# The last block's expert rows added by a 0/1 product, other blocks' rows during it, and z1 with its contraction outside

## What is computed

```
for l in range(2):
    h = rmsnorm(x, norm_mix[l])
    z = h @ w_in[l]                       # first 640 of its columns: "z1"; the other 800: "z2"
    ...                                   # two attentions, gates
    x = x + mix @ w_out[l]
    h = rmsnorm(x, norm_ffn[l])
    grp = argmax(h @ w_group + b_group)   # one group a token, so one row of results a token
    ...                                   # top 2 of the group's 8 experts, weights
    x = x + sum over the 2 experts of wt * ((silu(h @ w1[e]) * (h @ w3[e])) @ w2[e])
return rmsnorm(x, norm_final)             # x: 512 tokens x 1024
```

## Time and profile before

| | us |
|---|---|
| median of 3 runs (lowest, highest) | 2060.18 (2056.29, 2061.72) |
| profiled execution | 2053.19 |
| its span from the first to the last recorded instruction | 2051.5 |
| PE busy | 1942.0 |
| DVE, ACT busy | 1412.4, 1205.5 |
| mean DMA rate over the span | 252 GB/s |

### The profile page before, as it was taken

How to read it: one execution, slowest core, us unless ns; L and a number is a source line. 1 busy time by engine, 2 the same in 40 slices (tenths; PEclk the granted TensorE clock), 3 DMA queues, 4 the chain that set the end, 5 groups by cost and what they waited for, 6 DMA issues and landing times.

```text
span 2051.5 us, 27023 instructions
## 1 busy us (share of the span) xinstructions
PE 1942.0 (95%) x9266; PEld 1576.4 (77%) x9266; DVE 1412.4 (69%) x1792; ACT 1205.5 (59%) x1510; POOL 162.6 (8%) x175
## 2 busy tenths in 40 slices
PE   8979999999999999999688899999999999999994
PEld 6867777787888888888578677777888888888883
DVE  4344444468999899889544344436689998999895
ACT  4444444247777777777444444433477777777773
POOL 0000000022110111011000000000301100110010
PEclk9999999999999999999889999999999999999997
DMA  4234113549999999999421631135699999999992
GB/s 147 81 94 116 59 36 102 207 150 391 382 370 374 379 378 369 382 381 378 147 97 60 138 91 42 42 110 194 211 391 391 370 360 385 385 369 375 377 362 89
DMA packets 157960, 500.66 MB, mean 244 GB/s; under 512 B 22288, under 2 KB 38672, under 8 KB 157872
## 3 DMA queue, kind: packets, MB, share of 16 engines
q1 hardware_dynamic: 146192, 459.70, 60.8%
q0 software_dynamic: 11680, 39.80, 6.5%
HBM read 486.79 MB, written 29.63 MB: 252 GB/s over the span
## 4 chain that ended last, share of the span: by engine, by line
PE 90%; DVE 4%; ACT 2%; DMA 1%; issue 1%; POOL 0%; POOLq 0%; DVEq 0%; ACTq 0%; SPq 0%
PE ps L1449 27%; PE ps L1451 25%; PE ps L1450 25%; PE ps L1668 3%; PE ps L1600 2%; PE ps L1604 2%; PE ps L1654 1%; PE ps L1798 1%; DVE wl L1017 1%; ACT wh L666 1%; DVE wl L1012 1%; PE ps L1759 1%; PE ps L1713 1%; PE ps L1497 1%; PE ps L1771 1%
## 5 line engine op out<-in xcount | busy, mean ns | idle before, releaser
L1012 DVE TENSOR_TENSOR wl<-raw,wh 128x2048 fp32r<-128x2048 f32 (+1 forms) x402 | 907.5, 2279 | 186.3 <-ACT wh L665 183.7
L665 ACT ACTIVATE wh<-raw 128x2048 fp32r<-128x2048 f32 (+1 forms) x406 | 753.9, 1883 | 75.8 <-PE ps L1451 67.6
L1449 PE MATMUL ps<-wh,xgh 128*128 128x512 f32 x1024 | 414.2, 405 | 0.0
L1451 PE MATMUL ps<-wh,xgl 128*128 128x512 f32 x1024 | 402.4, 393 | 0.0
L1450 PE MATMUL ps<-wl,xgh 128*128 128x512 f32 x1024 | 401.3, 392 | 0.0
L1451 PEld LDWEIGHTS ps<-wh,xgl 128*128 128x128 f32 x1024 | 192.2, 188 | 43.5
L1450 PEld LDWEIGHTS ps<-wl,xgh 128*128 128x128 f32 x1024 | 192.8, 188 | 37.7
L1449 PEld LDWEIGHTS ps<-wh,xgh 128*128 128x128 f32 x1024 | 192.5, 188 | 37.9 <-issue 0.2
L1449 PE MATMUL ps<-wh,hth 128*128 128x512 f32 x512 | 200.9, 392 | 2.0 <-DVE htl L1035 2.0
L1451 PE MATMUL ps<-wh,htl 128*128 128x512 f32 x512 | 200.7, 392 | 0.0
L1450 PE MATMUL ps<-wl,hth 128*128 128x512 f32 x512 | 200.7, 392 | 0.0
(11 more groups left out here) (294 smaller groups left out, 2675.8 us busy)
## 6 DMA issues: line engine op xcount, KB each, us to landing
raw<-in_w SPq DMA_DIRECT2D x512, 512.0 KB, 6.1
raw<-in_w SPq DMA_DIRECT2D x128, 1024.0 KB
raw<-in_w_gate SPq DMA_DIRECT2D x16, 1024.0 KB
xslots<-zrow POOLq DMA_DIRECT2D x2, 6240.0 KB, 36.1
xg<-xslots POOLq DMA_DIRECT2D x16, 520.0 KB, 6.9
raw<-in_w_out SPq DMA_DIRECT2D x8, 1024.0 KB
raw<-in_w_in SPq DMA_DIRECT2D x8, 800.0 KB
raw<-in_w_oa SPq DMA_DIRECT2D x4, 1024.0 KB
```

Source lines behind the costliest of these rows:

```text
L665: return nc.scalar.activation(dst, src, ACT.Copy)
L1012: return V.tensor_tensor(dst, src, hi.bitcast(F32), ALU.subtract)
L1449: MM(dst, lh, rh, start=first, stop=False)
L1451: return MM(dst, ll, rh, start=False, stop=last)
```

## The change

The result rows of the last block no longer go through DRAM. `place` holds each token's slot less 896 (the last block's first slot). In the last block DVE compares a row 0..127 with it (`selection`), which gives a 0/1 matrix token x slot (`sel`); PE transposes it to bank 7 and ACT copies it to `selt`. At the block's end ACT rounds the 128 x 1024 rows to `yh` (`y_high`), DVE subtracts to `yl` (`y_low`), and PE multiplies `selt` with both, which puts each row at its token (`y_product`: 16 products of 128 x 512 into all eight banks). DVE adds the banks to `xl` (`add_half`).

The other blocks' rows are still written to `yrows`, which is now set to zero by a DMA in the attention part. During the last block GpSimd reads them tile by tile into `yb`, and DVE adds each to `xl` (`earlier_rows`), one after expert 3, 4, 5 and 6's first `up` unit; the next tile is read when the one before is added. `hi_unit(0)` and `lo_unit(0)` ahead of the last copies are gone.

z1 now runs k outside and the five column groups inside, and waits by k: `first_high(k)` and `first_low(k)` split one k of a unit and signal `hk_done`, `lk_done`. The transposed halves are renumbered: half c of tile t goes to bank 4c+t, and k 0 to 3 need only the halves c = 0. In layer 0 PE does 5 instead of 8 products with `ident`.

```diff
+                pool.dma_start(yrows, zrow[0, 0:D].partition_broadcast(T)).then_inc(S["zero_in"], 16)
...
-                n_blocks = blocks(pool, move_block)
-                pool.wait_ge(S["gath_in"], n_blocks * 16)
-                hold(n_blocks, 0)
-                nc.gpsimd.memset(ib[:, :], 0).then_inc(S["moe_done"], 1)
...
+                with pool.Fori(0, NG - 1) as b:
+                    move_block(b, b)
...
-                    pool.dma_start(y8[:, t, :], tiles(yrows)[:, t]).then_inc(S[f"y8_in{t}"], 16)
...
+                    if t:
+                        pool.wait_ge(S["xm_done"], t)
+                    pool.dma_start(yb[:, :], tiles(yrows)[:, t]).then_inc(S["y8_in"], 16)
...
+            def first_high(k):
+                n = first_unit(k)
+                if k == plan[n][1]:
+                    hi_room(n, 0)
+                for (gain, dst), (_, src) in zip(first_pieces(k, hi_at(n)), first_pieces(k, raws[rl_place(n)], True)):
+                    last = hi_part(dst, src, gain)
+                last.then_inc(S["hk_done"], 1)
...
+            def y_high(b):
+
+                act.wait_ge(S["used_m"], b * NU + NU)
+                for h in range(2):
+                    nc.scalar.activation(yh[:, h * 512:(h + 1) * 512], ps[5 + h][:, :], ACT.Copy
+                                         ).then_inc(S["yh_done"], 1)
...
+                if l:
+                    first_high(0)
                 square(0)
                 square(1)
                 root(0)
                 square(2)
                 root(1)
-                turned_high(0)
-                square(3)
-                root(2)
-                turned_high(1)
+                if l == 0:
+                    square(3)
+                    root(2)
+                turned_high(0, 0)
+                if l:
+                    square(3)
+                    root(2)
+                turned_high(0, 1)
                 root(3)
-                turned_high(2)
-                split_to(1)
-                turned_high(3)
+                turned_high(1, 0)
+                turned_high(2, 0)
+                if l == 0:
+                    first_high(0)
+                turned_high(3, 0)
+                first_high(1)
+                first_high(2)
+                for t in range(1, NT):
+                    turned_high(t, 1)
+                for k in range(3, KD):
+                    first_high(k)
                 split_to(U_Z1[1] + 1)
                 if l == 0:
                     act.wait_ge(trig_in, 2)
@@ -918,23 +962,25 @@
...
+                        if u == ("up", 4, 1) and not prepare:
+                            act.wait_ge(S["selt_ps"], b - (NG - 2))
+                            nc.scalar.activation(selt[:, :], ps[7][:, :], ACT.Copy).then_inc(S["selt_done"], 1)
...
-                    act.wait_ge(S["used_m"], n_blocks * NU + (hi_place(0) + 1 - NHI))
-                    hi_unit(0)
-                y_first(n_blocks - 1)
...
+            def y_low(b):
+                for h in range(2):
+                    dve.wait_ge(S["yh_done"], (b - (NG - 1)) * 2 + (h + 1))
+                    cols = slice(h * 512, (h + 1) * 512)
+                    V.tensor_tensor(yl[:, cols], ps[5 + h][:, :], yh[:, cols].bitcast(F32), ALU.subtract
+                                    ).then_inc(S["yl_done"], 1)
...
+            def add_half(b, t, h):
+                if (t, h) == (0, 0):
+                    dve.wait_ge(S["xm_done"], NT)
+                    dve.wait_ge(S["x8_done"], (b - (NG - 1)) * NT + BASE["x8_done"])
+                dve.wait_ge(S["yp_ps"], (b - (NG - 1)) * 2 * NT + (h * NT + t + 1))
+                cols = slice(h * 512, (h + 1) * 512)
+                last = V.tensor_tensor(xl[:, t, cols], xl[:, t, cols], ps[4 * h + t][:, :], ALU.add)
+                if h == 1:
+                    last.then_inc(S["x8_done"], 1)
...
+                add(0, 0)
+                add(1, 0)
+                add(0, 1)
+                add(1, 1)
                 mean(0)
-                add_y(2)
+                add(2, 0)
+                add(2, 1)
                 mean(1)
-                add_y(3)
+                add(3, 0)
+                add(3, 1)
                 mean(2)
-                turned_low(0)
-                mean(3)
-                turned_low(1)
-                split_to(1)
-                turned_low(2)
-                turned_low(3)
                 if l == 0:
-                    split_to(U_Z1[1])
+                    mean(3)
+                else:
+                    first_low(0)
+                turned_low(0, 0)
+                if l:
+                    mean(3)
+                turned_low(0, 1)
+                turned_low(1, 0)
+                turned_low(2, 0)
+                if l == 0:
+                    first_low(0)
+                turned_low(3, 0)
+                first_low(1)
+                first_low(2)
+                for t in range(1, NT):
+                    turned_low(t, 1)
+                for k in range(3, KD):
+                    first_low(k)
...
+                seq(V.tensor_scalar(place[:, :], slot[:, :], -float(P * (NG - 1)), None, ALU.add))
...
+                            V.tensor_scalar(sel[:, t, :], iota_p[:, :], place[:, t:t + 1], None, ALU.is_equal
+                                            ).then_inc(S["sel_made"], 1)
...
+                    def earlier_rows(t):
+
+                        dve.wait_ge(S["y8_in"], 16 * (t + 1))
+                        V.tensor_tensor(xl[:, t, :], xl[:, t, :], yb[:, :], ALU.add).then_inc(S["xm_done"], 1)
...
+                        if u == ("up", 2, 0) and not prepare:
+                            selection()
+                        if kind == "up" and 3 <= e < 3 + NT and half == 0 and prepared and not prepare:
+                            earlier_rows(e - 3)
...
-                    lo_unit(0)
-                y_second(n_blocks - 1)
...
-                    for _ in range(8):
+                    for _ in range(5):
...
-                        last = MM(ps[2 * t + k // 4][:, k % 4 * P:(k % 4 + 1) * P], xl[:, t, k * P:(k + 1) * P],
+                        last = MM(ps[4 * (k // 4) + t][:, k % 4 * P:(k % 4 + 1) * P], xl[:, t, k * P:(k + 1) * P],
...
+                for k in range(KD):
+                    n = first_unit(k)
+                    pe.wait_ge(S["lk_done"], k + 1)
+                    if k == 0:
+                        pe.wait_ge(S["h1l_done"], NT + 1)
+                    if k == KD // 2:
+                        pe.wait_ge(S["h1l_done"], 2 * NT)
+                    for m in range(AH // 2 + 1):
+                        last = mm3(ps[m][:, :], *part(n, k, m * P, P), h1h[:, k, :], h1l[:, k, :], k == 0, k == KD - 1)
+                        if k == KD - 1 and m < AH // 2:
+                            last.then_inc(S["z1_ps"], 1)
+                    if k == plan[n][1] + plan[n][2] - 1:
+                        last.then_inc(S["unit_used"], 1)
 
...
+                        if u == ("up", 3, 0) and not prepare:
+                            pe.wait_ge(S["sel_made"], (b - (NG - 2)) * NT)
+                            for t in range(NT):
+                                last = nc.tensor.transpose(ps[7][:, t * P:(t + 1) * P], sel[:, t, :], ident[:, :])
+                            last.then_inc(S["selt_ps"], 1)
...
+                def y_product(b):
+                    pe.wait_ge(S["selt_done"], b - (NG - 2))
+                    for h in range(2):
+                        pe.wait_ge(S["yl_done"], (b - (NG - 1)) * 2 + (h + 1))
+                        cols = slice(h * 512, (h + 1) * 512)
+                        for t in range(NT):
+                            tok = slice(t * P, (t + 1) * P)
+                            MM(ps[4 * h + t][:, :], selt[:, tok], yh[:, cols], start=True, stop=False)
+                            MM(ps[4 * h + t][:, :], selt[:, tok], yl[:, cols], start=False, stop=True
+                               ).then_inc(S["yp_ps"], 1)
```

More of the change, by code:

```diff
@@ L301, in hybrid_trunk @@
         m_names = """hi_m lo_m used_m routed gath_in xg_ps xgh_done xgl_done sig_done hw_done ht_ps hth_done htl_done
-            y_ev ib_done scat_done held wslot_done moe_done y8_in0 y8_in1 y8_in2 y8_in3 x8_done""".split()
+            y_ev ib_done scat_done held wslot_done place_done sel_made selt_ps selt_done
+            yh_done yl_done yp_ps y8_in xm_done x8_done""".split()
         S = {n: sem(n) for n in d_names}
@@ L368, in pieces, with first_unit, first_pieces @@
             return got
+        def first_unit(k):
+            return next(n for n in range(*U_Z1) if plan[n][1] <= k < plan[n][1] + plan[n][2])
+        def first_pieces(k, at, as_loaded=False):
+            n = first_unit(k)
+            return pieces(n, at, as_loaded)[2 * (k - plan[n][1]):2 * (k - plan[n][1]) + 2]
         def product_ready(eng, signal, m, groups, units):
@@ L396, in overflow, with chained_blocks @@
             return novf + NG
-        def blocks(eng, body):
-            with eng.Fori(0, NG) as b:
```

(15 more changed lines are left out.)

157 lines of the change are left out of this document (96 added, 61 removed).

## The result

The changed kernel takes 2041.44 us in the median of four runs (2040.19 to 2042.17) beside 2058.23 us for the kernel before in its own four (2053.50 to 2061.72): a ratio of 0.9916, with a 95% interval of 0.9897 to 0.9934. It is faster by 16.8 us. The forecast was 34.1 us and 2026; the range ended at 2040.

A forecast was written before the change was run, and what follows sets the result against it. PE, busy for 95% of the span, bounds the kernel, so only its waits can yield gains: 8.7 + 2.1 + 16.9 + 7.7 - 0.9 - 0.4 = 34.1 us. From a median of 2060.2 this gave 2026, range 2017 to 2040.

The forecast's parts named there:

- The start of layer 0: Up to z1 in layer 0: z1 starts at 16.6, gaining 8.7 us, and runs at full clock, 2.1 more.
- The chain of the seam: Between the layers, from block end E: products at E + 1.8, tiles E + 7.8, z1 E + 15.9; gain 16.9 us.
- The last block: In each layer's last block: DVE falls back 2 us against 4 of cover; transposes cost PE 0.44; tile reads land in time.
- the rival of late reads: Last blocks: reads of `yrows` land late and lateness adds up; 3.5 us a layer at landing time 9, 2033; chance 0.12.
- the small start: Start of layer 0: z1's units land together, z1 starts 2 to 5 us later, 2031; chance 0.1.
- the covered read-back: Between the layers: the read-back was covered anyway, so only the start gains, 2050; chance 0.03.
- PE's own walk through the overflow loop ... I take 0 and keep up to 2 for both places.: Before `y_product` at both block ends: PE's pass through the loop, charged 0, up to 2 us kept in the range.
- so I take it as held: Between the layers: full clock despite PE pauses of 1.8 and 2.3 us; slower tiles would cost 2.6.
- the clock in the gaps: Rival: clock drops in the gaps, tiles 2.6 us longer and z1's first k at half rate, 2030; chance 0.15.
- 2 MB of zeros written in the attention part, where the DMA queues are far from full; neither is on a path.: Attention part: zeroing `yrows`, and the 2 MB more read in the last block, were claimed off any path; no cost charged.
- the layers were taken as unchanged: Rest of the layers: no clock loss charged; small steps only, such as 0.2 us a layer for `place`.

The follow-up runs named there:

- start_only: Kernel before with only z1's new order, per-piece weight conversion and banks, and 5 ident products in place of 8: 2055.39 us, ratio 0.9948.
- The single branch: Changed kernel with one branch around PE's loop over overflow blocks, in place of a branch in each of three rounds: 2033.43 us, ratio 0.9884.
- before_zeroed: Kernel before with only the 2 MB zeroing of `yrows` added at the start of each layer: 2065.08 us, ratio 1.0029.
- held_zeroed: Kernel before with products without effect ahead of six PE waits per layer, plus the zeroing of `yrows` at the attention's start: 2057.02 us, ratio 0.9993.
- held_after: Changed kernel with products without effect ahead of six PE waits in each layer: 2029.37 us, ratio 0.9819.
- held_before: Kernel before with products without effect ahead of six PE waits in each layer: 2044.78 us, ratio 0.9893.
- late_zero: Changed kernel with the zeroing of `yrows` issued half way through the attention in place of its start: 2037.35 us, ratio 0.9907.
- held_late: Changed kernel with products without effect ahead of six PE waits per layer and the zeroing half way through the attention: 2018.64 us, ratio 0.9804.

## Why the prediction was wrong

**What held.** The start of layer 0 (10.2 of 10.8, and 11.2 in start_only's trace). The chain of the seam once PE is there: `yh`, `yl`, adds, tiles, z1. The last block, where the waits of DVE list the reads of `yb` with 1.1 us in three waits:

```profile
DVE xl L1499 <- DMA yb<-yrows: 1.1, 3, 0.4
```

PE stood still for none of it, so the rival of late reads is out. So are the small start and the covered read-back.

**The step that cost most of what is shown: "PE's own walk through the overflow loop ... I take 0 and keep up to 2 for both places."** It is 3.3 to 4.4 us of "issue" at each seam, beginning when the last product has run. Beyond `yl` this is 1.8 us. With it fell **"so I take it as held"**: PE paused 3.7 us before the selection products, not the 2.55 of the earlier trace rows, and 11 of 16 between the layers and 13 of 16 at the end ran at the low clock. Together 3.9 at the first seam and 3.5 at the end. The single branch gave 8.0 us back, and 5.7 and 6.2 with the clock held. The prediction had the clock in the gaps as a rival at 2030; its range kept 2 us for the walk where walk and clock took 7.4. The Trainium skill's figures for a branch (Advanced Engine Details and Errata, Control Flow Timing) would make the walk under 1 us, an estimate from the page; the measurement decides, and it is over three times that.

**Another step that failed: "2 MB of zeros written in the attention part, where the DMA queues are far from full; neither is on a path."** They were not far from full: the trace of the kernel before has DMA shares of 0.86 and 0.75 in the 40 us behind the old zeroing's issue. The new one kept them full for some 10 us longer; a gate load was late and ACT stood before it; in before_zeroed, held_zeroed and held_after PE then waited for the exponentials behind it. Cost: 6.7 us in the kernel before (interval 1.9 to 10.3), and some 11.5 in each of the two held kernels. In the changed kernel itself moving it gave 4.1, which is not clear of noise. The Trainium skill (DMA: Bandwidth & Descriptors, "Issuing engines are not separate DMA queues") says that transfers of different issuers run on the same 16 engines and interleave. The traces agree: zeros that GpSimd issued made loads that SyncE issued late, 6.0 us at ACT in held_zeroed against none in layer 0 of held_before.

**A third: the layers were taken as unchanged.** The sum was made against one execution. Its clock, 0.981, was one that only the two shortest of the 17 runs of before had; 2053.19 was no typical state from which to read that the layers cost no clock. 9.3 of the 17.3 us that are missing went in the layers, a part of it by the zeroing.

**The bill.** Predicted 34.1, measured 16.8. Of the 17.3 missing, 0.6 lies at the start and 7.4 at the seams; this part is shown. How the other 9.3 divide is not settled. late_zero would put 4 of them to the zeroing. The trace of the changed kernel puts them to falls of the clock behind waits that both kernels have, with no pause of PE for the zeroing; why all four runs of the changed kernel stood at a mean clock of 0.979 or 0.980, no better than before's typical 0.978, stays open. With the clock held the bill closes better: from held_before (2044.78) to held_late (2018.64) 26.1, beside the 27.4 read from the places of the change, and 6.2 more with the branch, 32.3 in all beside 34.1. These lie in two rounds; by the profiled spans, 2044.9 and 2017.2, the first part is 27.7.

## What to carry over

Cost a new transfer against the loads that run beside it in its own 50 us, and follow which instruction stands behind a late load on the engine that takes it; then put the transfer where the queues are empty, which cost one wait instruction here. Read the share of the queues in the slices where the transfer will stand, not over the stage. Control flow on the engine that bounds the kernel is work that the engine's own products do not hide: branch once around a rare loop. Where runs of one kernel spread, look at the mean granted clock of each run, and fill the bounding engine's short waits with products without effect before comparing versions: it took 21 us off the kernel before in its own round (13 beside its median in the others), and most of the spread, and it was what made the zeroing's cost visible. It also moves the work behind it, so what it shows must be looked for again in the kernel without it.

## What the runs showed of the hardware

- TensorE's walk through three rounds of a loop, each with a branch around a body that is not run, and the load of the count: 3.3 to 4.4 us of "issue" in which it does nothing (changed kernel 3.70 and 3.32, late_zero up to 4.4). Behind 15 products of 3.59 us put ahead of it, 3.46 were left between the layers and 2.23 at the end. With one branch around it, no time beyond a wait of 1.4 to 2.0 us for data.
- The same waits of TensorE, between 1.2 and 5 us long here, were followed by a fall of the clock from 2.4 to 1.2 GHz in some executions and not in others. The kernel before had 2052.67 us at a mean clock of 0.981 and 2068.98 at 0.971; with products ahead of six of them in each layer its four runs had 0.984 or 0.985.
- With products that add a zero column onto open sums among the added ones, held_late had a granted clock of 1.00 in the stretch from 330 to 480 us, which holds the output projection, where the changed kernel had 0.97.
- A DRAM write of 2 MB issued 0.9 us behind one of 6.2 MB by the same engine landed 44.1 us after its issue, 10 us after the larger one; issued after it, it landed in 12.7 us. The larger one took 34.7 us with it and 36.1 without.
